# Two transformer layers on one core: a unit's first products moved between the last ones of the unit before, input sums shared by two engines, a third weight sum on GpSimd, modulation work spread out

## The reference

```python
def swiglu(h, w_gate, w_up, w_down):
    return (jax.nn.silu(h @ w_gate) * (h @ w_up)) @ w_down

# first layer: spatial gating needs normalised values before its products
v = layernorm(v, g_v)
mixed = einsum('gts,bcsgd->bctgd', w, v_chunks) + b_s
# second layer
mod = jax.nn.silu(c) @ mod_w + mod_b      # 6 x 1024 columns, one row
shift1, scale1, gate1, shift2, scale2, gate2 = split(mod, 6)
h = rms_norm(x, g_pre_mix) * (1 + scale1) + shift1
```

## Time and profile before

| | |
|---|---|
| median of 3 runs | 1573.59 us (1573.15 to 1573.81) |
| profiled execution, its own time | 1574.16 us |
| its span, first to last instruction | 1572.4 us |
| PE busy | 1535.3 us, 98% of the span |
| DVE busy | 1020.2 us, 65% |
| ACT busy | 670.3 us, 43% |
| POOL busy | 669.1 us, 43% |
| mean granted clock of PE | 0.994 of full |

### The profile page before, as it was taken

The page is one execution under the profiler, slowest core; times in us unless marked ns, Lnnn a source line. Parts: engine busy times, 40 slices in busy tenths (PEclk is TensorE's granted clock), DMA queues, the critical chain, the costliest instruction groups (busy, mean ns, idle before and its releaser), DMA issues.

```text
span 1572.4 us, 23291 instructions
## 1 busy us (share of the span) xinstructions
PE 1535.3 (98%) x8908; PEld 1347.0 (86%) x8908; DVE 1020.2 (65%) x1385; ACT 670.3 (43%) x1107; POOL 669.1 (43%) x541
## 2 busy tenths in 40 slices
PE   9999999999998999999999999999999999999998
PEld 8878788887797999988898888888889799999886
DVE  4342676468567998964276979634446799897423
ACT  5223444323444454443176675332226444445221
POOL 3881002448624676658220811682002277663000
PEclk9999999999999999999999999999999999999999
DMA  7542132324532444454322221453232144444231
GB/s 210 165 136 80 54 81 55 121 82 132 175 94 68 113 131 126 128 170 126 126 89 81 70 65 55 128 157 116 80 107 81 54 135 124 119 132 138 94 107 54
DMA packets 189620, 171.40 MB, mean 109 GB/s; under 512 B 20688, under 2 KB 162000, under 8 KB 189520
## 3 DMA queue, kind: packets, MB, share of 16 engines
q1 hardware_dynamic: 181456, 144.84, 30.7%
q0 software_dynamic: 8064, 25.20, 5.3%
HBM read 167.91 MB, written 2.10 MB: 108 GB/s over the span
## 4 chain that ended last, share of the span: by engine, by line
PE 84%; POOL 6%; DVE 4%; issue 3%; ACT 1%; DMA 1%; SPq 0%; DVEq 0%; POOLq 0%; ACTq 0%
PE bank L2251 17%; PE bank L2253 17%; PE bank L2252 17%; PE bank L2345 6%; PE bank L2346 6%; PE bank L2347 6%; POOL mod_raw L940 2%; PE bank L2414 2%; PE bank L2413 2%; PE bank L2417 2%; POOL mod_acc L943 2%; PE bank L2564 1%; PE bank L2306 1%; DMA mod_raw<-in_mod_w 1%; PE bank L2319 1%
## 5 line engine op out<-in xcount | busy, mean ns | idle before, releaser
L1546 DVE TENSOR_TENSOR w_lo<-raw,w_hi 128x2048 fp32r<-128x2048 f32 (+1 forms) x109 | 214.3, 1967 | 234.2 <-ACT w_hi L1059 234.1
L2251 PE MATMUL bank<-h_hi,w_hi 128*128 128x512 f32 (+1 forms) x800 | 309.9, 387 | 3.6 <-DVE w_lo L1546 3.5
L2253 PE MATMUL bank<-h_hi,w_lo 128*128 128x512 f32 (+1 forms) x800 | 299.0, 374 | 0.0
L2252 PE MATMUL bank<-h_lo,w_hi 128*128 128x512 f32 (+1 forms) x800 | 298.9, 374 | 0.0
L1059 ACT CAST w_hi<-raw 128x2048 fp32r<-128x2048 f32 (+1 forms) x108 | 171.4, 1587 | 196.2 <-PE bank L2253 188.7
L940 POOL TENSOR_SCALAR mod_raw<-mod_raw,c_silu 128x512 f32<-128x512 f32 x96 | 189.5, 1974 | 42.2 <-DMA mod_raw<-in_mod_w 38.7
L2345 PE MATMUL bank<-s_hi,w_hi 128*128 128x256 f32 x576 | 167.8, 291 | 17.8 <-DVE silu_t L1767 10.8
L2251 PEld LDWEIGHTS bank<-h_hi,w_hi 128*128 128x128 f32 x800 | 151.1, 189 | 32.7 <-DVE w_lo L1546 5.0
L2253 PEld LDWEIGHTS bank<-h_hi,w_lo 128*128 128x128 f32 x800 | 151.1, 189 | 27.6
L2252 PEld LDWEIGHTS bank<-h_lo,w_hi 128*128 128x128 f32 x800 | 151.4, 189 | 27.2 <-issue 1.9
L2347 PE MATMUL bank<-s_hi,w_lo 128*128 128x256 f32 x576 | 164.7, 286 | 0.0
(11 more groups left out here) (474 smaller groups left out, 3381.5 us busy)
## 6 DMA issues: line engine op xcount, KB each, us to landing
raw<-in_w_in SPq DMA_DIRECT2D x102, 512.0 KB, 4.5
...
```

The costliest lines, as they stand in the source:

```text
L1546: ins = dve.tensor_tensor(w_lo[s][:, cols], raw[s][:, cols], w_hi[s][:, cols].bitcast(F32), ALU.subtract)
L2251: pe.matmul(o, st_hi, mv_hi, start=first, stop=False)
L2252: pe.matmul(o, st_hi, mv_lo, start=False, stop=False)
L2253: return pe.matmul(o, st_lo, mv_hi, start=False, stop=last)
```

## The change

- **PE order.** Product p1 of the next unit moves from behind p5 to between p4 and p5. Product p2 of the next unit moves from behind p3 to between p5 and p3.
- **DVE and ACT orders** in the block part follow: the product with p3's result moves one unit later, b22 moves from the end of a unit to its middle, and the lo part of the pair t3, t2 moves ahead of c22.
- **Weight sums.** t3 moves from DVE to POOL, where t3, t2 and t4 stand in a row.
- **Input sums.** DVE forms s1 alone, at once when the input is there and ahead of the first tile's product; POOL forms s3, s2 and s4. The splits of s1, s3 and of s2 with s4 are three steps on each of ACT and DVE.
- **Modulation.** A pair is now 16 steps behind one beginning (`mod_begin`), and each step issues the slab of the next one, across the middle of the pair too. Pair 1 is spread: 8 steps ahead of the layer norm roots, 5 behind the merge, the last 3 in the block part. Pair 2 begins in unit 1 and its steps run in units 2 to 17; pair 5 begins in unit 0 and its steps run in units 1 to 16. PE turns pair 0 inside the value projection instead of behind the attention.

```diff
@@ pe_order @@
-            yield "p1 0"
+            yield from ("p1 0", "p2 0")
             for m in range(BLOCKS):
-                yield from (f"{p} {m}" for p in ("p2", "p7", "p6", "p4", "p5"))
-                yield from [f"p1 {m + 1}"] if m + 1 < BLOCKS else []
+                ahead = m + 1 if m + 1 < BLOCKS else None
+                yield from (f"p7 {m}", f"p6 {m}", f"p4 {m}")
+                yield from [f"p1 {ahead}"] if ahead else []
+                yield f"p5 {m}"
+                yield from [f"p2 {ahead}"] if ahead else []
                 yield f"p3 {m}"
@@ POOL: one modulation pair @@
+            def mod_begin(pair):
+                wait(gp, mod_read, pair)
+                then(gp.memset(mod_acc[:], 0.0))
+                for which in range(2):
+                    col = 512 * MOD_PAIRS[pair][which]
+                    gp.dma_start(mod_acc[0:1, which, :], a["mod_b_2"][:, col:col + 512]).then_inc(mod_b_in, 16)
+                mod_slab(pair, 0)
             def mod_step(pair, i):
...
+                if i + 1 < 2 * KD:
+                    mod_slab(pair, i + 1)
                 gp.wait_ge(mod_w_in[s], 16 * (step // 2 + 1))
@@ POOL: blocks @@
                 then(gp.tensor_tensor(s3, h_quarter(h_hi, 0, 0), h_quarter(h_hi, 1, 0), ALU.subtract))
                 then(gp.tensor_tensor(s3, s3, h_quarter(h_lo, 0, 0), ALU.add))
                 gp.tensor_tensor(s3, s3, h_quarter(h_lo, 1, 0), ALU.subtract).then_inc(block_pool, 1)
+                wait_dve(gp, which, "s1")
+                gp.tensor_tensor(s2, s1, h_quarter(h_hi, 0, 0), ALU.subtract).then_inc(block_pool, 1)
+                wait_pool_sum(gp, which, 2)
+                then(gp.tensor_tensor(s2, s2, h_quarter(h_lo, 0, 0), ALU.subtract))
+                then(gp.tensor_tensor(s4, h_quarter(h_hi, 0, 1), s2, ALU.subtract))
+                gp.tensor_tensor(s4, s4, h_quarter(h_lo, 0, 1), ALU.add).then_inc(block_pool, 1)
+                if which == 0:
+                    mod_step(1, 13)
                 for m in range(BLOCKS):
...
+                    wait_operand_free(gp, n0, which, m, 2)
+                    gp.tensor_tensor(t3, quarter_of(n, 1, 1), quarter_of(n, 0, 1), ALU.subtract).then_inc(block_pool, 1)
                     wait_dve(gp, which, f"t1 {m}")
...
-                    if 1 <= m <= 2 * KD:
-                        mod_step(pair, m - 1)
+                    if which == 0:
+                        if m == 0:
+                            mod_step(1, 14)
+                            mod_step(1, 15)
+                        elif m == 1:
+                            mod_begin(2)
+                        else:
+                            mod_step(2, m - 2)
+                    elif m == 0:
+                        mod_begin(5)
+                    elif m <= 2 * KD:
+                        mod_step(5, m - 1)
@@ POOL: ahead of and behind the layer norm roots @@
+            mod_begin(1)
+            for i in range(8):
+                mod_step(1, i)
             for t in range(NT):
                 gp.wait_ge(var_ready, t + 1)
...
-            mod_pair(1)
+            gp.wait_ge(merged, KD)
+            for i in range(8, 13):
+                mod_step(1, i)
             post_norm(0)
@@ DVE: hidden @@
-                tile(n0, 0, 0)
-                split(n0 + 2)
                 dve.wait_ge(h_lo_done, 2 * KD * (c + 1))
                 then(dve.tensor_tensor(s1, h_quarter(h_hi, 1, 0), h_quarter(h_hi, 1, 1), ALU.add))
                 then(dve.tensor_tensor(s1, s1, h_quarter(h_lo, 1, 0), ALU.add))
-                then(dve.tensor_tensor(s1, s1, h_quarter(h_lo, 1, 1), ALU.add))
+                dve.tensor_tensor(s1, s1, h_quarter(h_lo, 1, 1), ALU.add).then_inc(block_dve, 1)
+                tile(n0, 0, 0)
+                split(n0 + 2)
...
@@ PE: value projection @@
+                    if c == 1 and j == 0:
+                        token_unit(n_va, h_hi, h_lo, 0, True, False, chunk_pace(1), tiles=range(0, 2))
+                        pe.wait_ge(c_kept, 4)
+                        mod_columns(0)
```

More of the change, by code:

```diff
@@ L652, in dve_order, with act_order @@
         def dve_order():
-            yield from ("s_sums", "t1 0", "t3 0", "pair 0", "s_lo", "s3_lo", "sums 0")
-            for m in range(BLOCKS):
-                if m == 0:
-                    yield from ("t4 0", "t1_lo 0")
-                ahead = m + 1 if m + 1 < BLOCKS else None
-                yield from [f"t1 {ahead}", f"pair {ahead}"] if ahead else []
-                yield f"z {m}"
-                yield from [f"t3 {ahead}"] if ahead else []
-                yield from (f"c21 {m}", f"c22 {m}")
-                yield from [f"{part} {ahead}" for part in ("sums", "t4", "t1_lo")] if ahead else []
-                yield f"m {m}"
-        def act_order():
-            yield from ("pair 0", "s_hi", "s3_hi", "sums 0", "p1 0")
+            yield from ("s1", "s1_lo", "s3_lo", "s24_lo", "t1 0", "pair 0", "sums 0", "t4 0", "t1_lo 0")
             for m in range(BLOCKS):
                 ahead = m + 1 if m + 1 < BLOCKS else None
-                yield from ("t4 0", "t1 0") if m == 0 else ()
+                yield from [f"pair {ahead}"] if ahead else []
+                yield from [f"m {m - 1}"] if m > 0 else []
+                yield from [f"t1 {ahead}"] if ahead else []
+                yield f"z {m}"
+                yield f"c21 {m}"
+                yield from [f"sums {ahead}"] if ahead else []
+                yield f"c22 {m}"
+                yield from [f"t4 {ahead}", f"t1_lo {ahead}"] if ahead else []
+            yield f"m {BLOCKS - 1}"
+        def act_order():
+            yield from ("s1_hi", "s3_hi", "s24_hi", "pair 0", "sums 0", "p1 0", "t4 0", "t1 0")
+            for m in range(BLOCKS):
+                ahead = m + 1 if m + 1 < BLOCKS else None
                 yield from [f"pair {ahead}"] if ahead else []
@@ L676, in act_order @@
                 yield f"gate {m}"
-                yield from [f"t4 {ahead}", f"t1 {ahead}", f"p1 {ahead}"] if ahead else []
+                yield from [f"p1 {ahead}", f"t4 {ahead}", f"t1 {ahead}"] if ahead else []
         DVE_AT = {step: n + 1 for n, step in enumerate(dve_order())}
@@ L1038, in _ @@
             post_norm(2)
-            blocks(n_up2, 1, 3, 5)
+            blocks(n_up2, 1, 3)
             mod_lo_part(5)
@@ L1846, in _ @@
             split(n_va + 2)
-            for j in range(2):
-                split(n_va + j + 1, chunk_pace(1))
+            split(n_va + 1, chunk_pace(1))
+            mod_columns(0, shift_col[0], False)
+            split(n_va + 2, chunk_pace(1))
             for s in range(len(ATT_TASKS) + 3):
@@ L2513, in mod_columns @@
             def mod_columns(pair):
-                pe.wait_ge(mod_summed, 2 * pair + 2)
+                pe.wait_ge(mod_summed, pair + 1)
                 if pair == 2:
```

159 lines of the change are left out of this document (77 added, 82 removed).

## The result

| | before | after |
|---|---|---|
| median | 1573.70 us (1573.15 to 1573.85) | 1597.26 us (1595.78 to 1598.15) |
| span of the profiled execution | 1572.4 us | 1594.1 us |
| PE busy | 1535.3 us | 1535.5 us |
| DVE busy | 1020.2 us | 990.5 us |
| POOL busy | 669.1 us | 752.0 us |

The account below looks back on a forecast made before the run. PE is busy 1535.3 of 1572.4 us, so only its standstill can change. Mixing -1.0, first stage +8.4 - 8.3, second +8.5 - 4.4 give +3.2 on 1573.6, rounded to 1577; 8-in-10 range 1561 to 1587.

Parts of the forecast that it names:

- The steady unit: Block parts: a unit, set by DVE and POOL, goes to 10.6 us; 0.5 lost in 14 units, 7 us a part.
- the wait at z: Block parts: PE would stand in front of p5, because z ends 6.3 us after p7 starts and p5 starts at 5.76.
- What goes in the block parts: Stalls near 511, 520, 604 and in the second part go; first part -8.3 us, second -4.4, unit losses included.
- The start of the stages: Feed-forward stages: DVE's s1 and POOL's s3 take turns, delaying the first product; +8.4 us in the first, +8.5 in the second.
- second stall of 1.8 or 1.3: Start of the stages: the second L1546 ends after PE wants it; 1.8 us in the first, 1.3 in the second.
- The roots: Layer norm roots: eight modulation steps ahead make them 6.6 us late, PE too, plus 1.5 for the clock: +8.1.
- 5: Rival, units with modulation: L940 excludes DVE for all its length, 1.1 us more a unit, 28 units: 1608; chance 0.02.
- something else, slower: Whole kernel: a slower outcome covered by neither the forecast nor the rivals; chance 0.05.
- 1: Rival, stage starts: DVE's sums fit the idle slot, starts 0.5 us late, not 8.4 and 8.5: about 1561; chance 0.13.
- 3: Rival, layer norm roots: in time, stall 3.5 us or less without a slow clock: 1571 or less; chance 0.06.
- 2: Rival, block parts: the unit falls to PE's pace, the 7 us a part go to 0: 1563; chance 0.13.
- 4: Rival, stage starts: POOL takes the first turn, PE stands 7.7 us, not 5.1, in both stages: 1582; chance 0.18.

Follow-up runs that it names:

- e1: The changed kernel with DVE's c22 of a unit ahead of the sums' lo part of the next one; ratio 1.0129 to the kernel before.
- e2: The changed kernel with sums t3 and t2 of units 1 to 7 in memory of their own; ratio 1.0137 to the kernel before.
- e9: The changed kernel without POOL's scaling and addition in the middle 14 modulation steps of pairs 2 and 5; ratio 0.9976 to the kernel before.
- e10: The kernel before with the changed kernel's modulation alone, six steps ahead of the layer norm roots and two right behind; ratio 0.9946.
- e13: The kernel before with the parts of hidden tiles 4 and 5 formed in unit 17 in place of unit 8; ratio 0.9975.
- e14: The kernel before with the new modulation, six steps ahead of the roots, and hidden tiles 4 and 5 in unit 17; ratio 0.9903, 1558.05 us.
- e7: The changed kernel with the input sums as the kernel before had them; ratio 1.0130 to the kernel before.

## Why the prediction was wrong

**The steady unit** is the step that failed. The trace is 18.4 us above the sum; the block parts are 21.0 above their terms, and the other terms give back 2.6. The method, DVE's loop with POOL's turns in it, was right: e1, e2 and e9 say so. But the rows above, start to start, give sums 1.14, c22 0.34, t4's lo 0.76, t1's lo 0.61, gate 1.44, addition 0.34, pair 1.13, p3's product 0.34, b22 1.37, t1 to POOL's t2 0.75, t2 1.43, t4 1.41: 11.06. Against my 10.65:

- I had counted t2 as a turn of 1.15 between b22 and t1. It can't begin before t1 has ended; DVE waits for it, so it costs its whole length and the handovers: 2.18 with t1, 0.43 more than the 1.75 of the sum. The order of the instructions was in front of me, and I summed as if it didn't matter.
- c22 was put beside POOL's work. It stands behind the wait, so its 0.34 counts.
- The scaling was charged 0.50. It took 0.16 of DVE's time, because c22 covered it; e1 took the cover away and got the 0.50 back.

So the first point is the whole error of the sum: the other two cancel (0.34 against 0.34), and 0.43 is about the 0.41 between 10.65 and 11.06. Then I rounded 10.65 to 10.6, took 11.0 for the upper bound (it was crossed), and charged 14 units a part; the stall is in all 17. That the sum for the kernel before came out near its 10.33 was no test of the new order: it adds up to 10.45, not the 10.4 written, and t1 lay elsewhere in it. 0.98 for 17 units is 16.7 a part in place of 7. I also looked for the wait at z, in front of p5, two products too early. That c22 ended "0.5 ahead of p3" rested on a loop of the wrong length.

**What goes in the block parts.** Of the 3.9 booked for each of the stalls at 604 and 1368 only half the cause was named. By e10, e13 and e14 the 3.8 is won only if the hidden tiles' parts move too. In the changed kernel these parts cost unit 8 1.2 us (12.25). Unit 2 of the first part, with the reading of pair 1, was charged 1; the same reading costs e14 2.4 (a unit of 12.47 against 10.08).

**The start of the stages** was right in the steps up to PE's stall: turns with DVE first, product at 455.40 (forecast 455.4), L1586's end at 462.2 (462.4), stalls of 4.43 and 6.61 (forecast 5.1, and 5.7 net of the old 1.6, so 7.3). Mis-sized was the rest: no second stall of 1.8 or 1.3 came. That the start of the blocks is late anyway I had booked twice over, as e7 shows.

**The roots** were right as a mechanism and small: a stall of 9.04 in place of 6.6, 11.4 with the clock in place of 8.1. In other runs the same eight steps gave 6.6 to 8.8; which meeting of steps and lo parts makes the difference was not followed. What is gained behind them was 9.7, forecast 9.1. (With three meetings of 1.5 the forecast's last step ends at 337.8, not 338.1.) So the mixing came out at +0.4 only with the help of the first 20 us.

**Rivals.** The time lies above every rival but 5, where the forecast had left 0.05 for something else, slower. 1 and 3 (sums in the idle slot, roots in time) didn't happen. 2 (unit at PE's pace) is what e9 shows without the steps. 4 (POOL first) didn't: DVE started at 447.56, POOL was held. 5, that the scaling excludes DVE for all its length, is refuted: the scaling of 1.57 held DVE 0.16 in after and 0.50 in e1. The Trainium skill ("SBUF — State Buffer", "Who interferes with whom") gives the shared pair of ports to whoever issues first for the whole instruction, and blocks the other. For two additions this trace agrees (3.31 in place of 1.23), for the scaling it doesn't.
